# Weight chunks at two alignments, an unscaled first norm and a re-ordered front in a two-block transformer kernel

## The chip, the cores and the metric

One core of one Trainium2 chip. The metric is the device time in microseconds of one execution. Before: 1409.45 us, the median of 3 runs (1404.42 to 1409.93).

## What is computed

Two transformer blocks over 256 tokens of 1024 features, all in float32. Cut to what matters:

```python
def first_block(x, ...):
    h = rms_norm(x, attn_norm)
    mq, mk, mv, dq, dk, dv = split(h @ w_in)             # six parts of 512 columns
    mq, mk, dq, dk = (apply_rope(rms_norm(p, gain), cos, sin) for p in ...)   # norms over heads of 64
    a_out = rms_norm(moba_attention(mq, mk, mv))         # 8 heads
    b_out = rms_norm(diff_attention(dq, dk, dv, lam))    # 4 heads, A1 - lam * A2
    x = x + concat(a_out, b_out) @ w_out
    return x + peer_ffn(rms_norm(x, ffn_norm), ...)      # 16 of 16384 experts for each of 8 heads

def second_block(x, mem, ...):
    h = rmsnorm(x, norm_mix_g)                           # conv, stick-breaking and retention branches,
    x = x + sum(gates * branches) @ w_o                  # from h @ w_in_2
    x = x + memory_attention(rmsnorm(x), rmsnorm(mem, norm_mem_g), w_q, w_kv, w_out)
    x = x + squared_relu_mlp(rmsnorm(x), w_up, w_down)
    return rmsnorm(x, final_g)
```

## The kernel before

Tokens lie on the 128 partitions in two tiles (`TT`). All dense weights come as one stream of 228 chunks of 128 x 1024 float32 (512 KB), in the order of the table `STREAM`. A chunk is loaded by the SP queue into one of `RING` = 4 slots. ACT then writes its rounded high part, `w_hi`, in fp32r (L1009), and POOL the rest, `w_lo = ring - w_hi` (L1360). For six chunks of w_in (3, 5, 9, 13, 17, 21, the list `DVE_CHUNKS`) DVE does the subtraction (L1494), and POOL only sets a mark with a memset (L1376), so that the semaphore `lo_made` counts in order. The activations are split in the same way into `hT_hi` and `hT_lo`. Each product is three fp32r matmuls (`product`, L579 to L581): hi·hi, hi·lo, lo·hi.

There are two kinds of chunk. In a *natural* chunk (w_in 24, w_out 8, xv 8, in_nat 20, w_o 8, xo 8, mlp_down 32) the transposed activations are the stationary operand, which is loaded, and 512 weight columns are moved: 12 matmuls of 512 columns. In a *transposed* chunk (the other 120) the weights are loaded, and 256 columns of `hT` are moved: 24 matmuls of 256. A slot is free for the next `w_hi` when PE has done its chunk (`chunk_done`), and for the next load when its low part is made. In the tensors before, the four slots of `w_hi` and of `w_lo` all start 64 bytes from a multiple of 128; hT and the arena start at a multiple of 128.

Each engine runs its own list, written out in one order, with semaphores between them. PE's results go to 8 PSUM banks, which `plan()` hands out in turn; `open_bank` waits until the last user has emptied a bank. The front of the program, which the change touches, is this:

1. `norm("attn")`: ACT sums the squares of x (L1040), POOL raises the mean to -1/2 (L1344), DVE scales x into `xn` (L1456), PE turns it (L657), ACT and DVE write hT_hi (L1031) and hT_lo (L1450).
2. w_in in six groups of four chunks. For groups 0 to 3 (queries and keys) ACT squares the two results (L1081), DVE sums them over heads of 64 (L1527), POOL raises to -1/2 (L1332, L1334: 128 x 16), and DVE does RoPE: products out of PSUM into `t1` and `t2` (L1540 to L1543), their sum `qn` (L1549), a low part, and the product with the head's factor into `proj1` (L1552, semaphore `roped`). Groups 4 and 5 are values, copied by ACT.
3. `norm("mem")` in the same way for the memory rows; then PE turns the heads into eight `qkT` halves and ACT copies them.
4. Twelve steps of attention (score, maxes, exps, turned probabilities, values), with four chunks of the memory keys (xk) between them, and `keep_busy` matmuls that PE does while it waits.
5. POOL's two powers for the norms of the attention's output (`att_sums`), with low parts around them; then w_out.

From there to the end the change touches only where `w_hi` and `w_lo` lie and how POOL's list is written: in long stretches POOL's low parts run in a `Fori` loop, four to a turn, with the wait in a register.

```python
if made[0] % RING == 0 and loops > 1 and made[0] > max(DVE_CHUNKS):
    with pool.Fori(made[0] // RING, made[0] // RING + loops) as it:
        for s in range(RING):
            lo_part(s, it * RING + s)
```

## Time and profile before

| | us |
|---|---|
| median of 3 runs | 1409.45 |
| lowest, highest | 1404.42, 1409.93 |
| the profiled execution | 1408.7 |
| its span | 1406.9 |
| mean granted TensorE clock | 0.975 |
| PE busy | 1249.2 (89%) |
| POOL busy | 922.4 (66%) |
| DVE busy | 831.0 (59%) |
| ACT busy | 609.8 (43%) |

The span is the profiled stretch, from the first to the last instruction; the time is the whole execution's. PE is TensorE's matmul side and PEld its weight loads, which run beside matmuls. A matmul's duration in the rows holds its pipeline, so neighbours overlap; the distance of two starts tells the pace. `bank` is PSUM, `stat` small per-row numbers, `arena` the big shared SBUF tensor, `c` the constants.

### The profile page before, as it was taken

The numbers are of one execution on the slowest core, as the hardware profiler recorded it, in microseconds if no ns is written. First come the engines' busy times: TensorE is split into PE (matmuls) and PEld (weight loads), VectorE is DVE, ScalarE is ACT, GpSimd is POOL, SyncE is SP. The second block draws the span as 40 slices with busy tenths as digits, with TensorE's granted clock in tenths as the row PEclk, the third lists the DMA queues.
The fourth block names the chain that finished last, engine by engine and source line by source line (L and its number), as shares of the span: only waits on it lengthen the run. The fifth ranks groups of instructions, "written<-read, shape, count | busy, mean of one in ns | idle before, by whom it ended". The sixth has DMA issues, their size and how long they took to land.

```text
span 1406.9 us, 17638 instructions
## 1 busy us (share of the span) xinstructions
PE 1249.2 (89%) x5982; PEld 883.1 (63%) x5982; DVE 831.0 (59%) x1535; ACT 609.8 (43%) x1291; POOL 922.4 (66%) x541
## 2 busy tenths in 40 slices
PE   6999989888888886777878888999999999999997
PEld 5768785443444542233333344789999988899886
DVE  6777478677777767876767654703652632277301
ACT  5456443443534443223233322547455345555432
POOL 5971875555766655644444452896968864799985
PEclk9999999999999999899989999999999999999999
DMA  6540579999999999999999996464536643465662
GB/s 251 162 135 31 186 276 385 426 420 425 427 425 426 425 425 427 427 426 427 428 426 425 413 427 290 141 209 131 186 121 202 210 126 120 135 188 187 203 197 93
DMA packets 72943, 400.69 MB, mean 285 GB/s; under 512 B 8096, under 2 KB 8352, under 8 KB 39712
## 3 DMA queue, kind: packets, MB, share of 16 engines
q0 software_dynamic: 36864, 268.45, 45.5%
q1 hardware_dynamic: 33696, 123.35, 26.6%
q10 hardware_dynamic: 2304, 7.85, 1.5%
q8 instruction: 47, 0.77, 0.2%
q14 instruction: 32, 0.26, 0.0%
HBM read 396.48 MB, written 3.15 MB: 284 GB/s over the span
## 4 chain that ended last, share of the span: by engine, by line
PE 32%; DMA 21%; POOL 18%; issue 16%; DVE 8%; ACT 4%; POOLq 0%; ACTq 0%; SPq 0%; DVEq 0%
DMA arena<-in_experts,arena 21%; POOL w_lo L1360 14%; PE bank L855 11%; PE bank L579 6%; PE bank L581 6%; PE bank L580 6%; DVE arena L1721 3%; POOL arena L1415 2%; POOL stat L1334 1%; PE bank L632 1%; ACT arena L1171 1%; ACT diag L1177 1%; DVE arena L1668 1%; DVE arena L1456 0%; ACT w_hi L1009 0%
## 5 line engine op out<-in xcount | busy, mean ns | idle before, releaser
L1360 POOL TENSOR_TENSOR w_lo<-ring,w_hi 128x1024 fp32r<-128x1024 f32 x222 | 570.6, 2594 | 140.4 <-ACT w_hi L1009 139.4
L855 PE MATMUL bank<-arena,diag 128*128 128x512 f32 x968 | 455.4, 621 | 92.7 <-ACT diag L1177 92.7
L1415 POOL DMA_INDIRECT arena<-in_experts,arena x242 | 294.0, 1215 | 237.9 <-PE bank L855 168.9
L1721 DVE CUSTOM_DVE_ANT_0 arena<-arena 128x1024 f32<-128x1024 f32 x242 | 326.8, 1362 | 165.4 <-DMA arena<-in_experts,arena 165.1
L855 PEld LDWEIGHTS bank<-arena,diag 128*128 128x128 f32 x968 | 184.9, 197 | 342.9 <-issue 203.0
L1009 ACT ACTIVATE w_hi<-ring 128x1024 fp32r<-128x1024 f32 x228 | 240.7, 1059 | 193.2 <-PE bank L581 130.6
L579 PE MATMUL bank<-hT_hi,w_hi 128*128 128x256 f32 x736 | 208.4, 283 | 5.5 <-DVE hT_lo L1450 2.7
L581 PE MATMUL bank<-hT_hi,w_lo 128*128 128x256 f32 x736 | 205.3, 279 | 0.0
L580 PE MATMUL bank<-hT_lo,w_hi 128*128 128x256 f32 x736 | 205.3, 279 | 0.0
L1168 ACT ACTIVATE arena<-arena 128x2 f32<-128x2 f32 (+2 forms) x99 | 20.2, 204 | 410.5 <-DVE arena L1721 410.4
L579 PEld LDWEIGHTS bank<-hT_hi,w_hi 128*128 128x128 f32 x736 | 138.0, 187 | 8.2 <-issue 6.9
L580 PEld LDWEIGHTS bank<-hT_lo,w_hi 128*128 128x128 f32 x736 | 138.3, 188 | 1.0 <-issue 1.0
L581 PEld LDWEIGHTS bank<-hT_hi,w_lo 128*128 128x128 f32 x736 | 138.0, 187 | 0.0
L579 PE MATMUL bank<-w_hi,hT_hi 128*128 128x512 f32 x272 | 115.6, 425 | 9.1 <-POOL stat L1376 3.5
L581 PE MATMUL bank<-w_hi,hT_lo 128*128 128x512 f32 x272 | 108.9, 400 | 0.0
L580 PE MATMUL bank<-w_lo,hT_hi 128*128 128x512 f32 x272 | 108.7, 400 | 0.0
L1177 ACT ACTIVATE diag<-c,arena 128x128 f32<-128x128 f32 x256 | 85.6, 392 | 3.2
L579 PEld LDWEIGHTS bank<-w_hi,hT_hi 128*128 128x128 f32 x272 | 51.9, 191 | 29.4 <-issue 6.9
L1022 ACT ACTIVATE arena<-bank 128x512 f32<-128x512 f32 (+2 forms) x78 | 42.3, 578 | 60.4 <-PE bank L581 38.4
L580 PEld LDWEIGHTS bank<-w_lo,hT_hi 128*128 128x128 f32 x272 | 52.1, 192 | 14.1 <-issue 2.9
L1171 ACT ACTIVATE arena<-arena 128x1 f32<-128x1 f32 x256 | 58.3, 285 | 5.3 <-DVE arena L1715 2.1
L581 PEld LDWEIGHTS bank<-w_hi,hT_lo 128*128 128x128 f32 x272 | 51.8, 190 | 12.8
(243 smaller groups left out, 1694.7 us busy)
## 6 DMA issues: line engine op xcount, KB each, us to landing
ring<-in_stream SPq DMA_DIRECT2D x228, 512.0 KB
arena<-in_experts,arena POOLq DMA_INDIRECT x242
kv_park<-arena ACTq DMA_DIRECT2D x8, 256.0 KB
arena<-kv_park ACTq DMA_DIRECT2D x1, 2048.0 KB, 7.9
x_res<-in_x SPq DMA_DIRECT2D x2, 512.0 KB, 5.2
arena<-in_mem SPq DMA_DIRECT2D x1, 1024.0 KB, 11.3
arena<-in_sub_keys ACTq DMA_DIRECT2D x1, 1024.0 KB, 5.8
out<-arena SPq DMA_DIRECT2D x2, 512.0 KB, 2.6
```

The costliest lines, as they stand in the source:

```text
L579: pe.matmul(out_, stationary[0], moving[0], start=start, stop=False)
L580: pe.matmul(out_, stationary[0], moving[1], start=False, stop=False)
L581: return pe.matmul(out_, stationary[1], moving[0], start=False, stop=stop)
L855: mm = pe.matmul(y_banks[half][:, :], diag[:, slot % DIAGS, :], rows_buf[BUFFER[slot]][:, D + 512 * half:D + 512 * half + 512], start=(i = ...
L1009: nc.scalar.activation(w_hi[:, c % RING, :], ring[:, c % RING, :], ACT.Copy)\
L1022: ins = nc.scalar.activation(dst, bank[:, 0:n] if src is None else src(bank), ACT.Copy, scale=scale)
L1168: own.link(nc.scalar.activation(g, dots[:, slot:slot + count], ACT.Gelu))
L1171: own.mark(nc.scalar.activation(w_slot[:, i % 16:i % 16 + 1], gelus[:, i % 16:i % 16 + 1], ACT.Copy, scale=gates[:, i:i + 1]))
L1177: nc.scalar.activation(diag[:, i % DIAGS, :], ident, ACT.Copy, scale=w_slot[:, i % 16:i % 16 + 1]).then_inc(S("diag_made"), 1)
L1360: nc.gpsimd.tensor_tensor(w_lo[:, slot, :], ring[:, slot, :], w_hi[:, slot, :].bitcast(F32), ALU.subtract).then_inc(S("lo_made"), 1)
L1415: nc.gpsimd.indirect_dma_start(out=rows_buf[b], out_offset=None, in_=experts, in_offset=bass.IndirectOffsetOnAxis(ap=expert_u[:, slot:slot ...
L1721: v.tensor_tensor_reduce(out=rows_buf[b][:, 0:D], in0=xn[:, slot // (PEER_H * PEER_K), :], in1=rows_buf[b][:, 0:D], scale=1.0, scalar=0.0, ...
```

## The change

**Addresses.** `w_hi` and `w_lo` get slots of 1040 words, and `shifted(c)` places chunk c: a natural chunk (`NATURAL`) starts at a multiple of 128 bytes, a transposed one 64 bytes from one, as before. The arena moves below x_res and the constants; the diag tiles start 64 bytes from a multiple of 128 where it was 32.

**First norm.** "attn" joins `UNSCALED`: PE turns x itself. The factor of the rows is left out of queries and keys, where the norm over heads takes it away but for the epsilon (`head_eps`), and is put on the values by ACT's copy.

**Head norms.** POOL's powers go. DVE makes the mean, ACT its square root, and DVE one refining step and a reciprocal. RoPE's first product and the sum stay in PSUM banks 5 and 6, the step in bank 7; w_in takes banks 0 to 4.

**Order.** The turned heads come in `TURN_ORDER`, four halves before the first scores and four after them; the memory norm moves into attention step 0, and ACT scales the memory rows. POOL makes low parts up to `w_out` + 2 before the first attention power, and one more before the second.

**Low parts.** POOL's loop is written out, one instruction to a chunk.

```diff
+HOME = 1040
+NATURAL = ("w_in", "w_out", "xv0", "xv1", "in_nat", "w_o", "xo", "mlp_down")
-UNSCALED = ("ffn", "xa", "mlp")
+UNSCALED = ("attn", "ffn", "xa", "mlp")
+ROPE_BANK, POWER_BANK = 5, 7
...
+            first = key[0] == "w_in" or key[:2] == ("attn", "hT")
+            bank = turn % (4 if among else ROPE_BANK if first else 8)
...
+TURN_ORDER = [(2, 0), (3, 0), (2, 1), (3, 1), (0, 0), (1, 0), (0, 1), (1, 1)]
...
-        line(16)
-        w_hi = tensor("w_hi", [RING, CHUNK], F32R)
-        w_lo = tensor("w_lo", [RING, CHUNK], F32R)
+        line(0)
+        w_hi_mem = tensor("w_hi", [RING * HOME], F32R)
+        w_lo_mem = tensor("w_lo", [RING * HOME], F32R)
...
+            wide = any(FIRST[name] <= c <= LAST[name] for name in NATURAL)
+            return HOME * (c % RING) + (16 if wide == bool(c % 2) else 0)
...
@@ PE
-            norm("attn", xn)
+            norm("attn", xs)
...
+            pe.wait_ge(S("roped"), 4)
+            turn_heads(TURN_ORDER[:4])
...
+                if step == 0:
+                    norm("mem", memn)
+                    turn_heads(TURN_ORDER[4:])
@@ ACT
+                if n < 4:
+                    hi_parts(FIRST["w_in"] + 4 * n + 3 + RING)
+                    act.wait_ge(S("head_means"), n + 1)
+                    nc.scalar.activation(head_root[n], head_mean[n], ACT.Sqrt, scale=0.25).then_inc(S("head_roots"), 1)
...
+            heads_out(TURN_ORDER[:4])
             norm_out("mem", con("g_mem"))
+            heads_out(TURN_ORDER[4:])
@@ POOL
-            for g in range(4):
-                lo_parts(FIRST["w_in"] + 4 * (g + 1) - 1 + RING + 1)
-                pool.wait_ge(S("head_sums"), g + 1)
-                rsqrt(hd_rs[g], hd_ss[g], 1.0 / 64, S("head_rstd"))
-            lo_parts(LAST["w_in"])
+            lo_parts(FIRST["w_in"] + 15)
             norm("mem")
-            lo_parts(LAST["xk"])
+            lo_parts(FIRST["w_out"] + 2)
             pool.wait_ge(S("att_sums"), 1)
             rsqrt(o_rs[:, 16:24], o_ss[:, 16:24], 1.0 / 128, S("att_rstd"))
-            lo_parts(FIRST["w_out"] + 2)
+            lo_parts(FIRST["w_out"] + 3)
@@ DVE
+                low_part(DVE_CHUNKS[2 + g])
...
+                for t in range(TT):
+                    turned = banks[ROPE_BANK + t][:, :]
+                    own.mark(v.tensor_tensor(turned, turned, t2[:, t * 512:(t + 1) * 512], ALU.add))
+                dve.wait_ge(S("head_roots"), g + 1)
+                own.link(v.reciprocal(head_step[g], head_root[g]))
+                own.link(v.scalar_tensor_tensor(head_step[g], head_step[g], 0.25, head_mean[g], ALU.mult, ALU.mult))
+                own.link(v.tensor_tensor(head_step[g], head_step[g], head_root[g], ALU.add))
+                own.link(v.reciprocal(head_power[g], head_step[g]))
```

How the lists move, at three places. First POOL in w_in, groups 1 and 2. Before (L1360 is a low part, L1376 the mark of one by DVE, L1332 and L1334 the power):

```order
L1376 MEMSET stat 128x1 [waits lo_by_dve]
L1360 TENSOR_TENSOR w_lo<-ring,w_hi 128x1024 [waits hi_made] x3
L1332 TENSOR_SCALAR stat<-stat 128x16 [waits head_sums]
L1334 TENSOR_TENSOR stat<-stat 128x16 [waits pool_own]
L1376 MEMSET stat 128x1 [waits lo_by_dve]
L1360 TENSOR_TENSOR w_lo<-ring,w_hi 128x1024 [waits hi_made] x3
L1332 TENSOR_SCALAR stat<-stat 128x16 [waits head_sums]
L1334 TENSOR_TENSOR stat<-stat 128x16 [waits pool_own]
```

and of the change (L1399 a low part, L1409 the mark):

```order
L1409 MEMSET stat 128x1 [waits lo_by_dve]
L1399 TENSOR_TENSOR w_lo<-ring,w_hi 128x1024 [waits hi_made] x3
L1409 MEMSET stat 128x1 [waits lo_by_dve]
L1399 TENSOR_TENSOR w_lo<-ring,w_hi 128x1024 [waits hi_made] x3
L1409 MEMSET stat 128x1 [waits lo_by_dve]
L1399 TENSOR_TENSOR w_lo<-ring,w_hi 128x1024 [waits hi_made] x2
```

The scalings and powers between the low parts are gone; the low parts keep their order.

Second, ACT from the end of w_in to the first exp of the attention. Before (L1031 is the memory norm's hT_hi, L1022 a copy of turned heads, L1098 the exp):

```order
L1031 ACTIVATE hT_hi<-bank,c_55 128x256 [waits result_done]
L1031 ACTIVATE hT_hi<-bank,c_55 128x256
L1031 ACTIVATE hT_hi<-bank,c_55 128x256 [waits result_done]
L1031 ACTIVATE hT_hi<-bank,c_55 128x256
L1031 ACTIVATE hT_hi<-bank,c_55 128x256 [waits result_done]
L1031 ACTIVATE hT_hi<-bank,c_55 128x256
L1031 ACTIVATE hT_hi<-bank,c_55 128x256 [waits result_done]
L1031 ACTIVATE hT_hi<-bank,c_55 128x256
L1022 ACTIVATE arena<-bank 128x512 [waits result_done] x8
L1098 ACTIVATE arena,stat<-arena,stat 128x128 [waits maxes,roped]
```

and of the change (L1048 copies, L1125 the exp of lambda, L1057 the memory norm's hT_hi):

```order
L1125 ACT_TABLE_LOAD
L1125 ACTIVATE stat<-stat 128x2 [waits lam_sums]
L1048 ACTIVATE arena<-bank 128x512 [waits result_done] x4
L1057 ACTIVATE hT_hi<-bank,c_56 128x256 [waits result_done]
L1057 ACTIVATE hT_hi<-bank,c_56 128x256
L1057 ACTIVATE hT_hi<-bank,c_56 128x256 [waits result_done]
L1057 ACTIVATE hT_hi<-bank,c_56 128x256
L1057 ACTIVATE hT_hi<-bank,c_56 128x256 [waits result_done]
L1057 ACTIVATE hT_hi<-bank,c_56 128x256
L1057 ACTIVATE hT_hi<-bank,c_56 128x256 [waits result_done]
L1057 ACTIVATE hT_hi<-bank,c_56 128x256
L1048 ACTIVATE arena<-bank 128x512 [waits result_done] x4
```

A table load and the exp of lambda have come in, and four of the eight copies stand ahead of the memory norm.

Third, POOL between attention and w_out. Before (L1332 and L1334 are the powers of the attention's norms):

```order
L1360 TENSOR_TENSOR w_lo<-ring,w_hi 128x1024 [waits hi_made] x4
L1332 TENSOR_SCALAR stat<-stat 128x8 [waits att_sums]
L1334 TENSOR_TENSOR stat<-stat 128x8 [waits pool_own]
L1360 TENSOR_TENSOR w_lo<-ring,w_hi 128x1024 [waits hi_made] x3
L1332 TENSOR_SCALAR stat<-stat 128x16 [waits att_sums]
L1334 TENSOR_TENSOR stat<-stat 128x16 [waits pool_own]
L1360 TENSOR_TENSOR w_lo<-ring,w_hi 128x1024 [waits hi_made] x6
```

and of the change (L1371 and L1373 the powers):

```order
L1399 TENSOR_TENSOR w_lo<-ring,w_hi 128x1024 [waits hi_made] x9
L1371 TENSOR_SCALAR stat<-stat 128x8 [waits att_sums]
L1373 TENSOR_TENSOR stat<-stat 128x8 [waits pool_own]
L1399 TENSOR_TENSOR w_lo<-ring,w_hi 128x1024 [waits hi_made]
L1371 TENSOR_SCALAR stat<-stat 128x16 [waits att_sums]
L1373 TENSOR_TENSOR stat<-stat 128x16 [waits pool_own]
L1399 TENSOR_TENSOR w_lo<-ring,w_hi 128x1024 [waits hi_made] x5
```

The three low parts that stood between the two powers (chunks 28 to 30) are now ahead of the first, and chunk 31's, which came behind the second, stands between them.

## Rows read from the trace of the kernel before

**Rows 1.** The page, part 1: busy time, share and instructions by engine
```profile
PE 1249.2 (89%) x5982; PEld 883.1 (63%) x5982; DVE 831.0 (59%) x1535; ACT 609.8 (43%) x1291; POOL 922.4 (66%) x541
```

**Rows 2.** Windows of natural-chunk stages: window, length, busy (xcount) by engine, clock, DMA
```profile
14.90:89.10 74.20, 70.59 (x290) 55.38 (x291) 57.96 (x69) 34.50 (x44) 64.71 (x35) 1.00 0.53 171
...
881.40:933.40 52.00, 51.38 (x216) 40.24 (x217) 23.59 (x12) 23.74 (x27) 49.11 (x19) 1.00 0.53 172
1121.50:1146.40 24.90, 22.20 (x88) 17.07 (x87) 10.76 (x13) 8.76 (x11) 14.86 (x7) 0.93 0.40 126
1191.70:1215.30 23.60, 22.87 (x98) 18.02 (x98) 2.96 (x6) 10.37 (x14) 14.68 (x7) 1.00 0.44 134
1309.20:1399.00 89.80, 89.80 (x386) 72.05 (x385) 10.27 (x8) 33.87 (x37) 75.96 (x34) 1.00 0.52 166
```

**Rows 3.** Timeline of PE in mlp_down: start, duration (us), line; thirteen matmuls
```profile
1345.65 0.39 PE L579 MATMUL bank<-w_hi,hidden_hl 128*128 128x512 f32 x1
...
1348.45 0.39 PE L579 MATMUL bank<-w_hi,hidden_hl 128*128 128x512 f32 x1
```

**Rows 4.** Timeline of PE in mlp_up, same columns; thirteen matmuls
```profile
1250.20 0.28 PE L579 MATMUL bank<-hT_hi,w_hi 128*128 128x256 f32 x1
...
1251.61 0.28 PE L579 MATMUL bank<-hT_hi,w_hi 128*128 128x256 f32 x1
```

**Rows 5.** Chain of waits in the gather: start, us, what
```profile
222.69 6.87 PE bank L855 x16
```

**Rows 6.** Timeline of all engines in the first 20 us, same columns
```profile
1.19 1.28 ACT L1040 ACT_TABLE_LOAD   x1 [1.19 <-PEq L2047]
...
5.55 1.06 ACT L1040 ACTIVATE arena<-x_res 128x1024 f32<-128x1024 f32 x1 [3.08 <-DMA x_res<-in_x]
...
8.20 2.25 ACT L1009 ACTIVATE w_hi<-ring 128x1024 fp32r<-128x1024 f32 x2 [0.22 <-DMA ring<-in_stream]
...
9.33 5.11 POOL L1360 TENSOR_TENSOR w_lo<-ring,w_hi 128x1024 fp32r<-128x1024 f32 x2
...
13.02 3.03 ACT L1031 ACTIVATE hT_hi<-bank,c 128x256 fp32r<-128x256 f32 x8 [2.57 <-PE bank L657]
...
14.99 0.76 PE L579 MATMUL bank<-w_hi,hT_hi 128*128 128x512 f32 x1 [0.73 <-DVE hT_lo L1450]
...
16.41 0.63 PE L579 MATMUL bank<-w_hi,hT_hi 128*128 128x512 f32 x1
...
16.83 0.63 PE L580 MATMUL bank<-w_lo,hT_hi 128*128 128x512 f32 x1
```

**Rows 7.** Timeline of POOL in w_in
```profile
53.84 8.10 POOL L1360 TENSOR_TENSOR w_lo<-ring,w_hi 128x1024 fp32r<-128x1024 f32 x3
...
63.17 3.87 POOL L1334 TENSOR_TENSOR stat<-stat 128x16 f32<-128x16 f32 x1
```

**Rows 8.** Timeline of DVE in w_in: the RoPE sum of group 0
```profile
33.47 3.10 DVE L1549 TENSOR_TENSOR arena<-arena 128x1024 f32<-128x1024 f32 x1
```

**Rows 9.** Waits of PE, 15 to 90 us: total, times, longest
```profile
PE bank L579 <- POOL stat L1376: 3.5, 3, 1.6
```

**Rows 10.** Timeline of ACT from w_in to the attention
```profile
94.51 4.06 ACT L1022 ACTIVATE arena<-bank 128x512 f32<-128x512 f32 x8
100.45 0.40 ACT L1098 ACTIVATE arena<-arena,stat 128x128 f32<-128x128 f32 x1 [1.88 <-DVE stat L1581]
```

**Rows 11.** Chain of waits between attention and w_out
```profile
138.00 7.97 POOL w_lo L1360 x3
...
146.34 2.92 POOL stat L1334
...
149.28 3.39 DVE arena L1628
```

**Rows 12.** Timeline of DVE between attention and w_out: the second att_sums
```profile
143.01 1.22 DVE L1622 TENSOR_REDUCE stat<-arena 128x16 f32<-128x1024 f32 x1 [1.21 <-ACT arena L1122]
```

**Rows 13.** Timeline of POOL in in_nat
```profile
884.29 45.87 POOL L1360 TENSOR_TENSOR w_lo<-ring,w_hi 128x1024 fp32r<-128x1024 f32 x17 [7.02 <-ACT w_hi L1009]
```

More of the change, by code:

```diff
@@ L148, in plan @@
     natural("w_in", 6, 4, FIRST["w_in"])
-    norm("mem")
-    for g in range(4):
-        for half in range(2):
-            add(("qkT", g, half))
+    for g, half in TURN_ORDER[:4]:
+        add(("qkT", g, half))
     for step in range(12 + 4):
@@ L161, in plan @@
                 add(("score", m))
+        if step == 0:
+            norm("mem")
+            for g, half in TURN_ORDER[4:]:
+                add(("qkT", g, half))
         if 3 <= step < 15:
@@ L384, in build, with shifted, w_part @@
         lo_mark = stats(6)
+        def shifted(c):
+            wide = any(FIRST[name] <= c <= LAST[name] for name in NATURAL)
+            return HOME * (c % RING) + (16 if wide == bool(c % 2) else 0)
+        def w_part(mem, c, cols=slice(0, CHUNK)):
+            return mem[:, shifted(c) + cols.start:shifted(c) + cols.stop]
         hT = [(hT_hi[:, k, :], hT_lo[:, k, :]) for k in range(KT)]
@@ L405, in build @@
         hd_ss = [stats(16) for _ in range(4)]
-        hd_rs = [stats(16) for _ in range(4)]
         nmax, psums, prec = stats(32), stats(32), stats(32)
@@ L410, in build @@
         ghead = stats(8)
+        head_eps = stats(TT)
+        head_mean, head_root, head_power = ([A(9216 + 64 * i + 16 * g, 16) for g in range(4)] for i in range(3))
+        head_step = [banks[POWER_BANK][:, 16 * g:16 * g + 16] for g in range(4)]
         gain_rows = A(7168, 1024)
@@ L673, in _, with turn_heads @@
             pe.wait_ge(S("c1_loaded"), 16)
-            norm("attn", xn)
+            norm("attn", xs)
             for n in range(6):
                 natural("w_in", 4, n, h_, FIRST["w_in"], normed("attn") if n == 0 else None)
-            norm("mem", memn)
-            for g in range(4):
-                pe.wait_ge(S("roped"), g + 1)
-                for half in range(2):
+            def turn_heads(order):
+                for g, half in order:
                     turn(("qkT", g, half), [proj1[g][:, t, p * P:(p + 1) * P]
                                             for p in (2 * half, 2 * half + 1) for t in range(TT)])
+            pe.wait_ge(S("roped"), 4)
+            turn_heads(TURN_ORDER[:4])
             def score(m, busy=0):
@@ L715, in memory @@
                 transposed_into(xk_bank[:, i % 2 * T:(i % 2 + 1) * T], FIRST["xk"] + i, None, h_)
-            for g in range(4):
-                normed("mem")(g)
             for step in range(16):
                 if step in KEY_STEPS:
+                    if step == KEY_STEPS[0]:
+                        for g in range(4):
+                            normed("mem")(g)
                     if KEY_STEPS.index(step) % 2 == 0:
@@ L1008, in hi_parts @@
                         act.wait_ge(chunk_done, c - RING + 1)
[L1009 removed]
+                    nc.scalar.activation(w_part(w_hi_mem, c), ring[:, c % RING, :], ACT.Copy)\
                       .then_inc(S("hi_made"), 1)
@@ L1462, in norm_low @@
                     split_lo((name, "hT", g), [hT_of[name][k] for k in ks], [gcol[:, k:k + 1] for k in ks])
-            def norm(name, src, dst, gcol):
-                for t in range(TT):
-                    scaled(name, t, src, dst)
-                norm_low(name, gcol)
             def add(key, t, cols):
@@ L1557, in _ @@
             own.link(v.tensor_scalar(lam[:, 5:6], lam[:, 4:5], -LAMBDA_INIT, None, ALU.add))
-            dve.wait_ge(S("mem_loaded"), 16)
-            norm("mem", mem, memn, con("g_mem"))
             mask = o_c2["mask"]
@@ L1582, in _ @@
                          .then_inc(S("maxes"), 1)
+                if step == 0:
+                    norm_low("mem", con("g_mem"))
                 if 1 <= step < 13:
```

99 lines of the change are left out of this document (51 added, 48 removed).

## The prediction

> **What bounds the kernel now.** I read the busy shares first: PE is busy for 89% of the span, POOL for 66%, no engine all the time [rows 1]. So the stages were read one by one in the windows. The middle of the run (about 200 to 870 us) is the expert gather; its DMA is full, and the change does not touch its data. The other stages are a stream of 228 weight chunks, in two kinds. In a *natural* chunk the weights are the moved operand (12 matmuls of 512 columns, 108 chunks), in a *transposed* one they are loaded (24 matmuls of 256 columns, 120 chunks). In the windows of the natural chunks PE is busy for nearly the whole stretch, also where POOL is not: in mlp_down 89.8 of 89.8 us, against 76.0 for POOL [rows 2]. There the spacing of matmuls is the time.
>
> That spacing: twelve natural matmuls start within 2.80 us, 0.2333 us each [rows 3]. At the clock level of 2.4 GHz 512 columns are 0.2133 us, so 0.020 us of each is something else. Twelve transposed matmuls take 1.41 us, 0.1175 each, where 256 columns are 0.1067 [rows 4]. The gather's fp32 matmuls, 512 columns out of addresses that are multiples of 128 bytes, take 6.87 us for sixteen, 0.4294 each, which is two times 0.2147 [rows 5]. At the 1.2 GHz level, in the first microseconds, natural matmuls are 0.42 to 0.43 apart, which is the bare 512 columns [rows 6]. So the extra 9% shows only where fp32r weights are moved at the full clock, from an address 64 bytes off.
>
> **The change part by part.** The sum is made against the profiled execution, 1408.7 us (span 1406.9 and 1.8 around it); the median of the runs shown is 1409.45, 0.75 more.
>
> *1. Start.* Now the squares (5.55), POOL's power, the scaling and two rounds of transposes come before the first matmul at 14.99 [rows 6]. Unscaled, PE turns tile 0 from 5.6 and tile 1 behind it; sixteen transposes are done by about 9. ACT is then the next late one: its first two chunks end at 8.20 + 2.25 = 10.45, and hT_hi follows, eight in 3.03 us, so the first pair at 11.2 and DVE's first low pair (0.9 behind) at 12.1. POOL's second low part ends at 9.33 + 4.7, and the first at 11.7. PE starts at 12.1: **−2.9 us**. Bounds: −1 (POOL's or the ring's order costs more) and −5 (the clock level also rises earlier, since PE turns tiles sooner).
>
> *2. w_in, POOL's powers.* POOL does three low parts in 8.10 us and then a power of 128x16 in 3.87 and its scaling (1.06), 13.1 us for four chunks, where PE needs 4 × 2.80 = 11.2 [rows 7]. PE's waits on this are 3.5 us, three times [rows 9]. The change gives the four powers to ACT (a square root of 16 elements) and DVE (four operations of 16 elements), so POOL has 8.1 us of work in 11.2: **−3.5 us**, bounds 0 and −4. What this puts on DVE: the sum of 1024 was 3.10 us while it read two SBUF operands beside POOL [rows 8] and is now two additions in PSUM of about 0.65, and the product likewise, so DVE's group stays near 10 us, just under PE's pace. Its low part of chunk 4g+9 is needed by PE some 4 us after it is made; that is the cover, and when it is gone PE waits (a rival below). ACT now waits for DVE's means before its next weight part; that part waits for PE for 2.8 us anyway.
>
> ACT also gets two table loads, since Sqrt and Exp alternate: the row of a load is 1.28 us [rows 6]. The first lies beside PE's work. The second stands on the path behind w_in and is in step 3. The Trainium skill (ScalarE: Activation LUTs, Table sets) speaks against this part: it asks to batch by set, since exp and then sqrt are two loads, some 2.66 us each with a drain. By the page step 3 would lose 1.4 us more. The trace has 1.28, and no drain can be told from its rows.
>
> *3. From w_in to attention.* Now the memory norm stands ahead of the heads: first exp at 100.45, 11.7 us behind the last w_in matmul at 88.7 [rows 2, 10]. After: two value copies (1.1), table load and exp (1.5), four copies at 0.51 (row: eight in 4.06), then PE's scores and sixteen transposes of mem, ACT's eight hT_hi (3.03) and four more copies, and then the first exp, at +11 to +12.5. PE however is ahead in the order: its scores and transposes of step 0 are done by +9.7, where all of them end at about +13 now, and it has less to wait for. The two nearly cancel: **−0.5 us**, bounds −2 and +2.6.
>
> *4. w_out.* POOL makes three w_out low parts (7.97) between the two powers, and the second power, the wait of DVE's scaling, starts only at 146.34 [rows 11]. After, these three are made in POOL's idle time before the first power and one, chunk 31's, of 2.4 us stands between; it can be done when DVE's second sums are, at 143.01 + 1.22 [rows 12]. **−2.0 us**, bounds 0 and −2.5.
>
> *5. Moved weights at a multiple of 128 bytes.* No row has an fp32r matmul of 512 columns moved from there. Bounds: 0.2147, the pace of one pass in rows 5, as the best, and 0.2533, the excess of 0.020 once more, as the worst, if the loaded hT at a multiple of 128 and the moved weights then meet in the memory. I take 0.2147: it is the nearest row with 512 columns moved from such an address. That is 12 × 0.0186 = 0.223 us a chunk: w_in 24 chunks −5.4; w_out 6 (two lie under a wait) −1.3; in_nat −3.0, as POOL's 17 low parts take 45.87 us from 884.29 on [rows 13], 2.70 each, so the last in_nat one ends at 927.5 and PE cannot end before 930.4 (now 933.4); w_o 7 −1.6; xo 8 −1.8; mlp_down 32 −7.1. Eight chunks of xv in the gather: 0, the gather's DMA covers them. **−20.1 us**. In mlp_down a chunk would take 2.58 and POOL's low part is 2.40 where DVE is quiet, so POOL is next, close behind.
>
> The Trainium skill (TensorE: Matmul & The Clock Gate, Back-to-back issue gap) gives N/2.4 + 2.5 ns, 0.2158 us for 512 columns, and knows no address. By the page the term would be 18.9 and not 20.1. Rows 3 disagree with it by 0.0175.
>
> *6. Loop written out, and the rest.* POOL's registers and branches go; low parts follow each other as closely without the loop (8.10 for three) as in it (45.87 for 17, beside DVE) [rows 7, 13]. 0. The diag tile starts 64 and not 32 bytes off; the gather waits for DMA, not for its weight load. 0.
>
> Sum: −2.9 − 3.5 − 0.5 − 2.0 − 20.1 = −29.0, so 1408.7 − 29.0 = 1379.7, and as a median 1380 us.
>
> **The rivals.**
>
> *A, the forecast*: 1380, with its own range 1371 to 1390, the low end by a start of −5, an attention of −2 and some better pace, the high one if half of step 5 comes.
>
> *B, the address does nothing for the moved operand.* For it: the transposed matmuls move hT from a multiple of 128 and yet are 10% over their columns [rows 4], so the excess may belong to fp32r at the full clock. Against: there the load of 128 columns takes as long as the matmul and can be the cause; in natural chunks it has twice the room, and the excess is there all the same. Then 1408.7 − 8.9 = 1400, with 1395 to 1405.
>
> *C, slower.* Loaded and moved operand both at a multiple of 128 collide. Now they are always 64 bytes apart, in both kinds, and this may be what keeps the excess at 9%. At 0.2533 each of some 95 chunks on the path costs 0.24 more, 22.8 us: 1408.7 − 8.9 + 22.8 = 1423. It decides from 0.2333 + 8.9/1140 = 0.241 us a matmul on; below that the front's gain pays for it. For it speaks only that the spacing is so regular; against it, that nothing in rows 5 suffers, though diag is loaded meanwhile.
>
> *D, DVE becomes the bound of w_in.* It keeps 10 to 12 us a group (RoPE through PSUM, four dependent small operations, a low part, the sum, the product) against PE's 10.3. If it needs 12.5, the low parts 17 and 21 come late and PE waits about 5 us: 1385, inside the range of A.
>
> *E, the front gives nothing* (the start bound by the ring's DMA, the root's wait holding ACT's weight parts): 1389 with step 5, 1409 without it.
>
> **How the numbers follow.** A with D 0.52, B 0.33, C 0.10, E without step 5 0.05. The measurement can tell about 0.5%, 7 us, from no change. Faster than 1402.4: A, most of B (0.30) and a slice of C and E (0.02): 0.84. Within 0.5%: the rest of B and E, 0.07. Slower: C, 0.09. The range takes A and most of B, **1371 to 1403**.
>
> **What would show it.** Spacing of twelve natural matmuls in mlp_down: 2.58 (A), 2.80 (B), over 2.9 (C). First w_in matmul near 12.1; no wait of PE on POOL's memset in w_in, whose last matmul is at about 76 (A) or 81 (B); spacing of transposed matmuls still 0.1175. First exp 11 to 12.5 behind w_in. Second att power near 144.3 less the front's gain. mlp_down from first to last 82 us and not 89. The forecast is wrong if the natural spacing stays, or if PE waits for low parts by DVE in w_in.

## The result and the profile after

The changed kernel takes 1417.7 us (median of 7 runs, 1414.91 to 1420.44) against 1409.45 (7 runs, 1404.42 to 1413.33): ratio 1.0052, 95% interval 1.0035 to 1.0069. It is half a per cent slower, where 1380 us (1371 to 1403) were forecast. Its profiled execution took 1417.7 us with a span of 1415.9; before, the span was 1406.9, so there are 9.0 us to find.

The page of the changed kernel, part 1, answers to [rows 1]:

```profile
PE 1256.9 (89%) x5982; PEld 890.4 (63%) x5982; DVE 829.5 (59%) x1564; ACT 614.1 (43%) x1299; POOL 892.0 (63%) x533
```

The shares say nothing: POOL is 30 us less busy, and the kernel is slower all the same. The windows by stage do tell. (in_gate is here the first 12 of its 24 chunks, up to a pause of 9.9 us that all the kernels have.) Columns as in [rows 2]; of the changed kernel w_in, in_nat, in_gate, w_o, xo, mlp_down, and last the gather from the first dot to the last:

```profile
12.30:80.50 68.20, 68.06 (x290) 55.39 (x291) 54.85 (x97) 37.74 (x50) 46.36 (x29) 0.98 0.63 203
881.40:933.40 52.00, 51.14 (x218) 40.17 (x219) 23.89 (x12) 23.81 (x27) 49.05 (x19) 1.00 0.55 171
998.10:1041.00 42.90, 35.87 (x293) 35.68 (x292) 30.87 (x21) 16.60 (x22) 28.75 (x12) 0.88 0.44 143
1124.80:1155.90 31.10, 25.66 (x100) 20.09 (x99) 14.24 (x15) 9.79 (x12) 17.03 (x8) 0.89 0.39 119
1202.00:1225.50 23.50, 22.72 (x100) 18.15 (x99) 3.01 (x6) 10.35 (x14) 14.75 (x7) 1.00 0.44 135
1319.20:1408.00 88.80, 88.80 (x387) 72.08 (x385) 10.63 (x8) 33.84 (x37) 76.27 (x34) 1.00 0.54 168
...
199.50:869.80 670.30, 561.70 (x1501) 270.90 (x1501) 475.73 (x1059) 240.34 (x721) 362.19 (x275) 0.93 1.00 416
```

The same two stretches of the kernel before that were not among its rows, in_gate and the gather:

```profile
999.20:1034.60 35.40, 34.62 (x293) 34.42 (x292) 25.86 (x21) 16.62 (x23) 31.12 (x12) 1.00 0.51 168
...
206.40:869.80 663.40, 551.95 (x1501) 265.55 (x1501) 478.25 (x1060) 240.45 (x721) 365.31 (x275) 0.95 1.00 420
```

Read one below the other: w_in is 6 us shorter than in [rows 2]. The gather begins 6.9 us sooner (199.5 against 206.4) and is 6.9 us longer, so its last dot starts at 869.8 in both kernels: the front's whole gain is gone there, at a full DMA that moves 416 GB/s instead of 420. in_gate is 7.5 us longer at a granted clock of 0.88, and w_o, from first to last matmul, 30.7 us against 26.9 (the window of [rows 2] begins inside the stage). From first to last matmul xo is 0.2 shorter and mlp_down 1.1. Stage by stage the books close: before in_gate −1.1, in_gate +7.6, up to w_o −0.8, w_o +3.8, up to mlp_down +0.7, mlp_down −1.1, together +9.1 of the 9.0.

Inside in_gate one wait does it, shown by the waits of all engines from 1015 to 1030 us (waiting engine and line, what it waited for, total, times, longest), and the chain there (start, us, what):

```profile
PE bank L596 <- DVE arena L1880: 7.0, 1, 7.0
```

```profile
996.59 4.96 DVE arena L1859
1001.57 3.48 DVE arena L1862 x4
1005.07 6.01 DVE arena L1866 x4
1011.11 8.27 DVE arena L1870 x4
1019.41 3.32 DVE arena L1873
1022.75 2.72 DVE conv_hl L1874
...
1026.64 0.56 DVE arena L1880
1027.24 0.58 PE bank L596
1027.82 0.21 PE bank L597
1028.03 0.21 PE bank L598
```

PE waits for a bank that holds the retention scores (L1880). DVE empties it only after its whole convolution, because that is the order of its program. The convolution's operations of 254 columns take 0.48 us alone and 2.6 when they meet a POOL low part: L1870 is four of them in 8.27 us. After the gap the matmuls are 0.21 us apart and not 0.113: the 1.2 GHz level. In w_o it is the same pair of engines, on DVE's timeline (start, us, what):

```profile
1118.93 2.52 DVE L1934 CAST hT_hi<-arena 128x512 fp32r<-128x512 f32 x1
1121.49 2.78 DVE L1935 TENSOR_TENSOR hT_lo<-arena,hT_hi 128x512 fp32r<-128x512 f32 x1
...
1124.90 2.19 DVE L1931 TENSOR_TENSOR arena<-arena 128x512 f32<-128x512 f32 x1
1127.13 2.47 DVE L1934 CAST hT_hi<-arena 128x512 fp32r<-128x512 f32 x1
1129.64 2.71 DVE L1935 TENSOR_TENSOR hT_lo<-arena,hT_hi 128x512 fp32r<-128x512 f32 x1
```

and on PE's, where the last three rows are 0.43 apart (the 1.2 GHz level again, as in [rows 6]):

```profile
1132.50 0.77 PE L596 MATMUL bank<-w_hi,hT_hi 128*128 128x512 f32 x1 [4.66 <-DVE hT_lo L1935]
1133.06 0.63 PE L597 MATMUL bank<-w_lo,hT_hi 128*128 128x512 f32 x1
1133.49 0.63 PE L598 MATMUL bank<-w_hi,hT_lo 128*128 128x512 f32 x1
```

Last, the spacing of mlp_down, answering to [rows 3], one matmul in three:

```profile
1351.27 0.39 PE L596 MATMUL bank<-w_hi,hidden_hl 128*128 128x512 f32 x1
...
1353.98 0.39 PE L596 MATMUL bank<-w_hi,hidden_hl 128*128 128x512 f32 x1
...
1356.74 0.40 PE L596 MATMUL bank<-w_hi,hidden_hl 128*128 128x512 f32 x1
...
1359.54 0.40 PE L596 MATMUL bank<-w_hi,hidden_hl 128*128 128x512 f32 x1
```

Twelve matmuls take 2.71 us in one place and 2.80 in another. Averaged by chunk, the whole stage repeats with a period of four chunks: 226.7, 232.7, 233.3, 227.9 ns. (The first matmul or two of a chunk still have the spacing of the chunk before, hence 227.9 and 232.7.) Four is the number of ring slots, so the spacing belongs to the slot, two quick and two slow.

### The profile page after: what moved, and what is told of

It is laid out like the page before. It is cut to its first block, busy times and chain, and to the rows that moved or that the text cites. A ratio compares the mean times of both kernels' runs of the same rounds, so it can differ in the third digit from the quotient of the medians.

```text
span 1415.9 us, 17416 instructions
## 1 busy us (share of the span) xinstructions
PE 1256.9 (89%) x5982; PEld 890.4 (63%) x5982; DVE 829.5 (59%) x1564; ACT 614.1 (43%) x1299; POOL 892.0 (63%) x533
## 4 chain that ended last, share of the span: by engine, by line
PE 51%; DMA 20%; DVE 12%; POOL 8%; ACT 5%; issue 4%; ACTq 0%; SPq 0%; POOLq 0%; DVEq 0%
DMA arena<-in_experts,arena 20%; PE bank L881 11%; PE bank L596 11%; PE bank L598 11%; PE bank L597 11%; POOL w_lo L1399 5%; DVE arena L1761 4%; POOL arena L1443 2%; PE bank L649 1%; PE bank L658 1%; ACT w_hi L1035 1%; ACT arena L1210 1%; ACT diag L1216 1%; PE bank L1006 1%; DVE arena L1870 1%
## 5 line engine op out<-in xcount | busy, mean ns | idle before, releaser
L1399 POOL TENSOR_TENSOR w_lo<-ring,w_hi 128x1024 fp32r<-128x1024 f32 x222 | 564.7, 2568 | 190.5 <-ACT w_hi L1035 189.8
L881 PE MATMUL bank<-arena,diag 128*128 128x512 f32 x968 | 466.7, 635 | 91.1 <-ACT diag L1216 91.0
L1443 POOL DMA_INDIRECT arena<-in_experts,arena x242 | 288.5, 1192 | 247.2 <-PE bank L881 171.2
L1761 DVE CUSTOM_DVE_ANT_0 arena<-arena 128x1024 f32<-128x1024 f32 x242 | 322.1, 1343 | 174.5 <-DMA arena<-in_experts,arena 174.3
L881 PEld LDWEIGHTS bank<-arena,diag 128*128 128x128 f32 x968 | 190.3, 202 | 347.5 <-issue 213.0
L1048 ACT ACTIVATE arena<-bank 128x512 f32<-128x512 f32 (+2 forms) x74 | 40.2, 570 | 59.1 <-PE bank L598 39.9
L598 PEld LDWEIGHTS bank<-w_hi,hT_lo 128*128 128x128 f32 x272 | 52.0, 191 | 12.1
```

What stands on the lines that cost most here:

```text
L598: return pe.matmul(out_, stationary[1], moving[0], start=False, stop=stop)
L881: mm = pe.matmul(y_banks[half][:, :], diag[:, slot % DIAGS, :], rows_buf[BUFFER[slot]][:, D + 512 * half:D + 512 * half + 512], start=(i = ...
L1048: ins = nc.scalar.activation(dst, bank[:, 0:n] if src is None else src(bank), ACT.Copy, scale=scale)
L1399: nc.gpsimd.tensor_tensor(w_part(w_lo_mem, c), ring[:, c % RING, :], w_part(w_hi_mem, c).bitcast(F32), ALU.subtract).then_inc(S("lo_made"), 1)
L1443: nc.gpsimd.indirect_dma_start(out=rows_buf[b], out_offset=None, in_=experts, in_offset=bass.IndirectOffsetOnAxis(ap=expert_u[:, slot:slot ...
L1761: v.tensor_tensor_reduce(out=rows_buf[b][:, 0:D], in0=xn[:, slot // (PEER_H * PEER_K), :], in1=rows_buf[b][:, 0:D], scale=1.0, scalar=0.0, ...
```

## The experiments

Twelve kernels in three groups, each measured beside the kernel before on the same chip. A reader of the texts on record needs one convention: addresses "modulo 256 bytes" are counted there from the kernel's first array. In the built program that array lies at 16512, itself 128 bytes past a multiple of 256, so "128 modulo 256" there is a true multiple of 256, and "a multiple of 256" there is 128 bytes off. Differences between two addresses are not touched by this.

| kernel | edit | this, us | before, us | ratio, interval |
|---|---|---|---|---|
| e1_all64 | changed, all chunks at 64 | 1418.74 | 1411.01 | 1.0056, 1.0043 to 1.0069 |
| e2_all128 | changed, all chunks at 0 | 1412.94 | 1411.01 | 1.0010, 1.0001 to 1.0019 |
| e4_all64_loop | e1 with POOL's loop | 1416.25 | 1411.01 | 1.0047, 1.0028 to 1.0065 |
| e5_arena | changed, arena 128 bytes on | 1405.59 | 1411.01 | 0.9956, 0.9941 to 0.9970 |
| b1_before_arena | before, arena 128 bytes on | 1419.24 | 1409.83 | 1.0069, 1.0046 to 1.0091 |
| e3_before_written | before, loop written out | 1411.36 | 1409.83 | 1.0008, 0.9996 to 1.0019 |
| e6_same256 | e5, moved chunks at the residue of hT | 1400.94 | 1409.83 | 0.9949, 0.9929 to 0.9969 |
| e7_pause | e5, one pause of POOL | 1403.10 | 1409.83 | 0.9957, 0.9941 to 0.9972 |
| e8_pause3 | e6, three pauses of POOL | 1397.74 | 1411.11 | 0.9909, 0.9889 to 0.9929 |
| e9_rs_first | e6, DVE's order in in_gate | 1397.55 | 1411.11 | 0.9914, 0.9901 to 0.9926 |
| e10_both | e8 and e9 | 1391.01 | 1411.11 | 0.9872, 0.9855 to 0.9889 |
| e11_front_alone | front only, layout of before | 1404.23 | 1411.11 | 0.9960, 0.9947 to 0.9973 |

### The place of the arena

The change moves the 128 KB arena ahead of x_res, and with it the buffers that the gathered rows land in. The edit of **e5_arena**:

```diff
+        place[0] += 32
         arena_at = place[0]
         arena = tensor("arena", [32768])
```

> The changed kernel with the arena, into which the gathered rows land, moved by 128 bytes in SBUF, to the same residue (128 modulo 256 bytes) as before the change. Arena theory: an 8192-byte packet of the gather goes back from 314 to 310 ns and the last dot from 869.8 to about 863 us, so the total to about 1410. Run-to-run theory (the transfers' rate belongs to the run or the chip): packets stay where those of the other kernels of this call are, total within 2 us of 1417.7.

The last dot is at 862.1 us, where 863 was expected, 7.7 sooner than in the changed kernel. The ratio falls by more, from 1.0052 to 0.9956: in_gate took 39.0 us in this profile and 42.5 in that one, which belongs to the stalls below. Beside it **b1_before_arena**, the same step in the other direction in the kernel before:

```diff
-        line(0)
+        line(32)
         arena_at = place[0]
```

> The kernel before with only its arena moved on by 128 bytes, from 128 modulo 256 bytes to a multiple of 256. Arena theory: the gather's 8192-byte packets go from 310 to 314 ns, the last dot from 869.8 to 877 to 879 us, the total to about 1416 to 1418 (in mlp_down the spacing may fall, next sentence). Residue theory of the spacing (a moved chunk is quick when its address modulo 256 bytes less that of the loaded operand is 0 or 64, slow at 128 or 192): mlp_down, whose hidden rows lie in the arena, goes from .2333 to .2290, -1.6 us; in_nat, whose operand is not in the arena, stays .2333. If the front was what slowed the gather: 1409 to 1411.

It came as the arena theory had it: 1419.24 us, last dot at 880.5. (It also starts the gather 2.2 us late, at 208.6.) The stretch from the first dot to the last, over all profiled runs:

| arena | kernels | first to last dot, us |
|---|---|---|
| at a true multiple of 256 bytes | before, e3, e5 to e11 | 661.7 to 663.4 |
| 128 bytes off | changed, b1, e1, e2, e4 | 670.4 to 672.9 |

Fourteen traces, no overlap, about 9 us apart. Windows of b1 and of e5 over the gather (columns as above):

```profile
208.50:881.80 673.30, 555.03 (x1504) 267.25 (x1504) 481.59 (x1061) 241.35 (x724) 365.92 (x275) 0.94 1.00 414
```

```profile
199.20:863.40 664.20, 555.11 (x1505) 267.96 (x1504) 481.64 (x1061) 241.30 (x723) 360.22 (x275) 0.94 1.00 420
```

The busy times of PE, DVE and ACT are the same to 0.1 us (POOL's, which also issues the gather, differs by 5.7); the length and the GB/s differ. The packets of 8192 bytes, 33,061 to 33,064 in each trace, take on average over the run 0.3156 us in the changed kernel and in b1, 0.3121 before, 0.3117 in e5 and 0.3114 in e11. The Trainium skill (DMA: Bandwidth & Descriptors, How a descriptor splits into AXI transactions) says, in words about reads, that a descriptor is cut at multiples of 256 bytes and that one which starts off such a multiple fetches from the multiple below it. If a landing address counts in the same way, an 8192-byte row takes 33 transactions and not 32, an estimate of up to 3%. The traces agree in direction, with 1.1% a packet; where in the transfer it is lost, no run here shows.

### The addresses of moved and loaded operands

**e1_all64** and **e2_all128** put all chunks at one offset:

```diff
-            return HOME * (c % RING) + (16 if wide == bool(c % 2) else 0)
+            return HOME * (c % RING) + (0 if c % 2 else 16)
```

and for e2 the last line reads

```diff
+            return HOME * (c % RING) + (16 if c % 2 else 0)
```

> The changed kernel with every split chunk 64 bytes from a multiple of 128, as before the change; all else as changed. Loop theory (POOL's written-out low parts shift its phase against DVE and hold the convolution and the w_o stage): nothing comes back by this, 1417 to 1420, mean matmul spacing of mlp_down .2333. Address theory (the mixed addresses themselves upset the stages): 1405 to 1410, with the 7.2 us gap before in_gate's end (1019.9 us) gone. My term 5 as measured in the changed kernel's trace (.2300 against .2333 where operands move) says 2 to 3 us slower than the changed kernel: 1420.

> The changed kernel with every split chunk at a multiple of 128. If the address acts only on chunks that are moved, the natural stages keep .2300 and the transposed ones (chunk loaded) keep .1133 to .1178: time within 2 us of 1417.7. If an address at the multiple hurts the loaded chunk, mlp_up's mean spacing grows over .1178 and the time by 1 us per 1.1 per cent of its 90 us.

e1: 1418.74, so nothing comes back, and the address theory of the stage losses falls. But mlp_down repeats 229.2, 228.9, 232.4, 233.3 ns over its four chunks, which .2333 everywhere (my expectation) is not. e2: natural chunks as in the changed kernel, but transposed ones went to 118.5 to 120.0 ns on average, and mlp_up to 91.8 us from 90.3: a *loaded* chunk at a multiple of 128 bytes is slower by 1.7%. By slots it is about 118.5 in 1 and 2, which lie 128 bytes from the moved hT modulo 256, and about 119.9 in 0 and 3, which lie at distance 0. hT itself is at a multiple of 128 in every kernel, so no run parts the chunk's own address from its distance to hT. (e2's median is nevertheless lower than e1's. Its profiled run has no stall in in_gate, and the runs of e1 scatter by 10 us; see below.)

The quick slots are known by one number: the address of the moved chunk less that of the loaded operand, modulo 256 bytes.

| difference | seen in | ns a matmul |
|---|---|---|
| 0 | changed, slots 0 and 3; e5, slots 1 and 2; e6, all | 226.7 |
| 64 | e1, slots 0 and 1; b1's mlp_down, all | 228.9 |
| 128 | changed, slots 1 and 2; e5, slots 0 and 3 | 233.3 |
| 192 | before, all; e1, slots 2 and 3 | 233.3 |

The slots are 4160 bytes apart in the changed kernel, 64 more than a multiple of 256, so offsets that are all multiples of 128 are still two residues modulo 256. In e5 the hidden rows moved by 128 bytes and quick and slow slots changed places. b1 had been foretold: its hidden rows moved from difference 192 to 64, .2290 expected, .2289 measured. The last step was **e6_same256**, with every natural chunk at difference 0:

```diff
-HOME = 1040
+HOME = 1024
...
-        line(0)
-        w_hi_mem = tensor("w_hi", [RING * HOME], F32R)
-        w_lo_mem = tensor("w_lo", [RING * HOME], F32R)
-        line(0)
+        place[0] += 32
+        w_hi_mem = tensor("w_hi", [RING * HOME + 16], F32R)
+        place[0] += 48
+        w_lo_mem = tensor("w_lo", [RING * HOME + 16], F32R)
+        place[0] += 48
...
-            return HOME * (c % RING) + (16 if wide == bool(c % 2) else 0)
+            return HOME * (c % RING) + (0 if wide else 16)
...
-                        act.wait_ge(chunk_done, c - RING + 1)
+                        act.wait_ge(chunk_done, c - RING + 1 + int(c % RING < 3 and shifted(c) > shifted(c - RING)))
```

The added words put w_hi, w_lo, hT and the arena all at one residue. A transposed chunk reaches 64 bytes into the next slot, so ACT waits for one chunk more where such a chunk follows a natural one.

> The changed kernel with the arena at 128 modulo 256 bytes, and every moved chunk, in all four slots, at the same residue modulo 256 as the operand loaded beside it (loaded chunks 64 bytes further; the slots no longer spread by 64 bytes). Residue theory: spacing .2267 in all slots of mlp_down (after: .2267 in two slots of four, .2333 in the two others), mlp_down 87.1 to 87.3 us against 88.3, all natural stages together -3 us: about 1402. If the alternation over the slots has another cause (the 4160-byte stride, the bank): still .2300 on average, 1405 to 1406.

All slots of mlp_down stand at .2267 from the fifth chunk on. Two rows of its timeline, twelve matmuls apart:

```profile
1345.34 0.39 PE L598 MATMUL bank<-w_hi,hidden_hl 128*128 128x512 f32 x1
...
1348.06 0.39 PE L598 MATMUL bank<-w_hi,hidden_hl 128*128 128x512 f32 x1
```

mlp_down is 87.1 us from first to last matmul (changed 88.3, before 89.4), and the median 1400.94. The ratios of e6 and e5, 0.9949 and 0.9956, are not told apart; what shows the rule is the spacing and the length of the stage.

### The written-out loop and the front, each alone

**e4_all64_loop** is e1 with the removed Fori loop back; **e3_before_written** is the kernel before without it:

```diff
-                    loops = (last + 1 - made[0]) // RING
-                    if made[0] % RING == 0 and loops > 1 and made[0] > max(DVE_CHUNKS):
-                        with pool.Fori(made[0] // RING, made[0] // RING + loops) as it:
...
-                        made[0] += RING * loops
-                    elif made[0] in DVE_CHUNKS:
+                    if made[0] in DVE_CHUNKS:
```

> The changed kernel with every chunk at 64 bytes and with POOL's loop for the low parts back: what is left of the change is the unscaled front and the place of the arena. Loop theory: the gap before in_gate's end goes from 7.2 to about 1 us and the w_o stage's losses (3.8 us) go, leaving only the slower gather against the front's gain: 1406 to 1410. If the loop is innocent (phase by the front): like e1, 1417 to 1420.

> The kernel before with POOL's low parts written out and nothing else. My term 6: 0, so 1409 to 1412 beside a before of 1411. Rival (the written-out row is quicker to start and so holds DVE's convolution longer): in_gate's gap grows from 0.9 to 4 to 7 us, 1415 to 1418.

e4 is 1416.25 (e1: 1418.74) and e3 has 1.0008, with 1 in its interval; e3's gap in in_gate (the longest distance of two matmuls less the usual one) is 0.93 us, before 0.94. The loop is innocent, and my first theory of the stage losses falls with it. e4's seven runs go from 1408.6 to 1421.0, e1's from 1410.2 to 1420.2, far more scatter than the 5.7 us over 18 runs of the kernel before on the same chip. The profiled runs of both were the fastest, and their in_gate had a gap of 0 (e4) and 1.4 us (e1), not 7.

**e11_front_alone** keeps all that the change does to the front; chunks, strides and loop are those of before, and so is the residue of every array modulo 256 bytes but that of the diag tiles (192 for 160). The arena stays ahead of x_res, at a true multiple of 256.

> The unscaled front alone: chunks, low-part loop and the residues of every array modulo 256 bytes as in the kernel before. My terms 1 to 4 give -8.9; the changed kernel's trace has the gather begin 6.9 us sooner, so 1403 beside a before of 1410, last dot at 863. If the front itself costs something later (another phase of POOL against DVE), the gain at the gather is there and part of it is lost behind 930 us: 1405 to 1410.

1404.23 against 1411.11, −6.9 us: most of what the front gives at the gather is kept to the end. In the profiled executions it is −7.3 at the first dot (199.1), −9.0 at the last (860.8) and −5.5 at the end of the span; w_o is 1.4 us longer, as it is in e3. The gap in in_gate is 0.92 us, as before. So the front alone does not bring the two long stalls; the rest of the change took its gain.

### DVE against POOL's low parts

**e7_pause** takes e5 and makes POOL wait once:

```diff
                 pool.wait_ge(S("hi_made"), c + 1)
+                if c == FIRST["w_o"] + 2:
+                    pool.wait_ge(S("merged"), 4)
```

> The kernel e5_arena with one wait more: POOL makes the low part of w_o's third chunk only when DVE has made all four pairs of merged rows. Port theory (a DVE operation of 0.43 to 0.69 us that meets a POOL low part takes 2.5 to 2.8 us, and this alone makes the gap of 4.7 us in w_o and the half clock behind it): DVE's operations there take 0.43 to 0.69 us, the gap goes, 1398 to 1400. If DVE is late there for another reason: gap stays over 4 us, or a wait on low parts takes its place, 1405 or more.

DVE's timeline of e7 in that stage, with POOL silent from 1109.9 to 1118.1:

```profile
1113.55 0.69 DVE L1934 TENSOR_TENSOR arena<-arena 128x512 f32<-128x512 f32 x1
1114.28 0.43 DVE L1937 CAST hT_hi<-arena 128x512 fp32r<-128x512 f32 x1
1114.74 0.69 DVE L1938 TENSOR_TENSOR hT_lo<-arena,hT_hi 128x512 fp32r<-128x512 f32 x1
```

The three took 2.19, 2.47 and 2.71 us in the changed kernel. The port theory of the durations is right, and my price for the fix was wrong: the time is 1403.1 and not 1398 to 1400, and by the ratios (0.9957, e5 0.9956) the pause gained nothing, because a wait on the low part takes the place of the wait on DVE:

```profile
PE bank L597 <- POOL w_lo L1402: 4.4, 2, 3.6
```

PE is through with the second chunk at 1116.5, and POOL may start the third one's low part only at 1117.9. The Trainium skill (SBUF — State Buffer, Who interferes with whom) says that a DVE instruction with two SBUF inputs, or a copy in a fast mode, and a GpSimd instruction that reads SBUF shut each other out for a whole instruction. The rows agree: 0.43 becomes 2.5 us, which is POOL's 2.4, and the evacuation that reads a PSUM bank (0.68) is never stretched. Hence **e8_pause3**, on top of e6, with POOL's pauses only as long as PE can bear:

```diff
+                if 2 <= c - FIRST["w_o"] <= 4:
+                    pool.wait_ge(S("merged"), c - FIRST["w_o"])
```

> The kernel e6_same256 with POOL's low parts of w_o's third, fourth and fifth chunks each waiting for DVE's pair of merged rows of that number less one (2, 3 and 4 pairs made), instead of e7's one wait for all four. Port theory: every DVE operation of a pair is 0.4 to 0.7 us or held once at most, no gap over 1.5 us in w_o, no half clock there, w_o 24 to 25.5 us against 29.8: 5 us off, about 1397. If low parts then come too late (as e7's gap of 3.8 us shows can be), the gap only moves: 1400 to 1402.

w_o is 26.1 us from first to last matmul (e6: 29.8), its longest gap 1.47 and its granted clock 1.00; the median is 1397.74, and by the ratios it is 0.4% under e6. The expected 5 us came as 3.7 in the stage. Its profiled run was one of 1405.93 us and had the other stall: PE waits 7.2 us in in_gate.

**e9_rs_first** goes at that one, by DVE's order alone:

```diff
+            for h in range(4):
+                bank = take(dve, ("rs", h))
+                v.tensor_tensor(sT[:, h, :], bank[:, 0:SC], o_c3["decay"][:, h * SC:(h + 1) * SC], ALU.mult)\
+                 .then_inc(evac_sem(("rs", h)), 1)
             for c in range(6):
                 wait_evacuated(dve, ("in_conv", c))
             u = cv[:, 1]
...
-            for h in range(4):
-                bank = take(dve, ("rs", h))
-                v.tensor_tensor(sT[:, h, :], bank[:, 0:SC], o_c3["decay"][:, h * SC:(h + 1) * SC], ALU.mult)\
-                 .then_inc(evac_sem(("rs", h)), 1)
```

> The kernel e6_same256 with DVE's four evacuations of the retention scores moved ahead of its convolution. Order theory (in_gate's gap of 1 to 7 us, different from run to run, is PE waiting for a bank that DVE frees only behind the convolution, whose operations POOL's low parts hold): no gap in in_gate over 0.3 us, and e6's two groups of times (1398 to 1401, 1406 to 1408) become one: 1397 to 1400. If the gap has another releaser it stays, with both groups.

1397.55, five runs between 1396.81 and 1400.23, where e6 had ten in two groups (six at 1398.1 to 1401.2 and four at 1406.0 to 1407.9). Five runs alone could miss the slower group by luck; the trace is the better witness: no gap is left in in_gate. The convolution is as slow as it was, but nobody waits for it.

> Both edits of e8_pause3 and e9_rs_first together. If they touch different stalls they add up: 1392 to 1395. If the time saved at one comes back as another wait, no better than the better of the two.

**e10_both**, the two edits together: 1391.01, ratio 0.9872. They add up. Windows of in_gate and w_o:

```profile
987.70:1020.70 33.00, 33.00 (x293) 33.00 (x292) 32.69 (x19) 16.64 (x22) 29.36 (x12) 1.00 0.57 185
1105.30:1131.90 26.60, 23.45 (x101) 17.84 (x100) 11.58 (x14) 8.76 (x11) 15.71 (x7) 1.00 0.43 135
```

PE is busy 33.0 of 33.0 us in in_gate (changed: 35.87 of 42.90), and the clock is 1.00 in both stages (changed: 0.88 and 0.89). DVE is busy for 32.69 us in in_gate, more than in the changed kernel (30.87), and it costs nothing. This version beats both kernels: 1.3% under the one before.

## Why the prediction was wrong

The forecast was −29.0 us, the profiled executions differ by +9.0, and 38 us are to be accounted for. About 17 of them are step 5, 11.4 are two stalls that no step had, 6.9 are the gather, and about 3 are the front. Step by step:

- **1, the start** (−2.9): first w_in matmul at 12.44, forecast 12.1, −2.55. Right. The clock's earlier rise, which was in the bounds only, came too: the matmuls 0.427 apart end at 15.5 and not at 19.4, some 0.7 us inside w_in.
- **2, POOL's powers** (−3.5): PE's waits on POOL in w_in [rows 9] are gone, 3.5 us. Right. Rival D, DVE as the bound of w_in, did not come: PE has no gap over 0.6 us between 12.44 and 80.06.
- **3, w_in to attention** (−0.5, bounds −2 and +2.6): wrong in size and sign. The first exp is at 92.90, 12.8 behind the last w_in matmul (forecast 11 to 12.5, before 11.7), and then the clock fell, which I had not in the sum. The window from 92.9 to 105.0 has a granted clock of 0.72, the same stretch before 1.00:

```profile
92.90:105.00 12.10, 12.10 (x59) 9.16 (x58) 6.36 (x19) 5.16 (x20) 2.41 (x1) 0.72 0.15 43
```

```profile
100.45:110.00 9.55, 9.55 (x57) 7.02 (x57) 7.13 (x22) 4.49 (x15) 2.42 (x1) 1.00 0.09 24
```

  0.28 × 12.1 = 3.4 us, and the lead over the kernel before shrinks from 8.7 at the end of w_in to 4.6 at DVE's second att sums (138.37 against 143.01): step 3 is +4, of which 1.1 is the later exp and the rest the clock. The fall does not come in every execution. Of the eleven profiled kernels with the new front, e1, e7 and e10 kept 1.00 from w_in to w_out; the window 80 to 140 us of the changed kernel and of e1:

```profile
80.00:140.00 60.00, 55.60 (x366) 45.98 (x366) 40.35 (x106) 39.04 (x109) 17.33 (x11) 0.94 0.23 71
```

```profile
80.00:140.00 60.00, 55.58 (x380) 46.21 (x379) 41.57 (x109) 39.35 (x110) 20.57 (x11) 1.00 0.25 81
```

  These three start the first dot at 196.9 to 197.8, the other eight at 199.1 to 200.6. Ahead of the exp PE waited 0.52 and 1.35 us in the changed kernel, and just as long in e1 and e7, so those two waits do not decide it. What does was not found.
- **4, w_out** (−2.0): the second power now starts 0.1 us behind the end of its sums (139.68). Before, it stood 1.8 behind them, low parts in between (146.05 in POOL's timeline against 144.23 [rows 12]): −1.7. Right.

  Up to here 8.9 were forecast without the address. At the first dot 6.9 arrive, of which about 1.2 is the address's (w_in and w_out), so the front gave 5.7 in this execution. e11, which has the front alone, is 6.9 us faster at the end.

- **The sentence that failed** stands outside the numbered terms: "its DMA is full, and the change does not touch its data". It moves the arena, and so the start of every gathered row, off a multiple of 256 bytes: +6.9 us here, about 9 between the two groups of traces. I had read that line of the diff as bookkeeping and priced it at nothing without a sentence. e5 and b1 show it in both directions.
- **5, the address** (−20.1): mis-sized by its row and wrong in its rule. I took .2147 from fp32 matmuls [rows 5]; fp32r ones stood at .2267 at best. (The formula that the prediction takes from the Trainium skill, TensorE: Matmul & The Clock Gate, Back-to-back issue gap, is given on that page for an isolated matmul and not for a stream, so it was no ground for this term.) And what counts is not the address of the moved chunk but its distance from the loaded operand's, modulo 256: the changed kernel has the good distance in half its slots only. Measured, the mean spacing of the natural stages fell from 233.3 to between 230.2 and 230.9 ns: −0.9 us for the 288 matmuls of w_in, −0.3 in w_out, −0.2 in each of in_nat (PE's busy time), w_o and xo, −1.1 in mlp_down, about −3 in all. e6 about doubles it. Rival B (nothing, .2333) was nearer. The time lies near rival C's 1423, but by luck: its cause (collision, over .241) did not come for moved chunks; e2 shows something of the kind, in small, for the loaded ones.
- **6, the loop** (0): right, e3.
- **What was in no step**: in_gate +7.6 and w_o +3.8. Both stalls were there before ([rows 2] has w_o at a clock of 0.93, and in_gate had a gap of 0.9 us); they hang on how DVE's short operations and POOL's low parts happen to meet. That DVE's order makes the one and POOL's low parts the other is shown by e9 and e8. Why they grew goes by the pace of the transposed chunks, as far as traces tell: 113.3 ns a matmul for long stretches and not 117.8, so that a chunk takes 2.72 us and leaves 0.3 us beside POOL's 2.4, where it was 2.83 and 0.4. In w_o all eleven traces without a pause of POOL agree: the longest gap is 4.7 to 4.9 us where the chunks ahead of w_o ended at 113.3 (changed, b1, e1, e4, e5, e6, e9), and 2.1 to 2.2 where they ran at 117.8 or slower (before, e2, e3, e11). b1 is the kernel before with its arena moved, so w_o's stall does not need the changed chunks. In in_gate the gap is 0.9 to 1.1 with the first eight chunks at 117.8 (before, b1, e3, e11, e6), 4.1 and 4.4 with four of them at 113.3 (e7, e5) and 7.2 and 7.4 with all eight (changed, e8), but 1.4 and 0 in e1 and e4, which also ran all eight at 113.3; e2, at 118.5 to 120.0, has 0.1. So this link is read from traces, has two exceptions and was not tested by itself, and what picks the pace stays open.

In one line: −6.9 at the first dot, +6.9 in the gather, +11.4 in the two stalls, and −2.3 in all other stages.

## What to carry to other kernels

When an edit reorders a memory layout, list every array whose address moves and who touches it, DMAs first: here one line moved the landing place of 268 MB, and 128 bytes cost 9 us. Where a matmul's pace matters, look at it chunk by chunk; a period equal to the number of buffers points at their addresses, and the average hides it. And before a stage is priced by its steady pace, ask which stall in it depends on the meeting of two engines: put what PE waits for ahead of what nobody waits for in the other engine's order, and let a helper that runs ahead pause while the late one works.

## What was not expected of the hardware

- Matmuls of fp32r with 512 moved columns are 226.7, 228.9, 233.3 and 233.3 ns apart as moved less loaded address is 0, 64, 128 and 192 modulo 256 bytes.
- Those with 256 moved columns have two paces, 113.3 and 117.8 ns, in one and the same kernel with one and the same layout. The kernel before runs the fifth to the eleventh chunk of mlp_up at 113.3 and all from the twelfth on at 117.8, and in in_conv it goes from 113.3 to 117.8 behind the fourth chunk. There each change stands at a break of PE's stream, of 0.03 to 0.55 us; but the changed kernel also goes from 117.8 to 113.3 at the end of the fourth chunk of in_sqk, where no distance is over 0.12 us. With the loaded chunk at a multiple of 128 bytes (e2) both are gone and it is 118.5 to 120.0. What picks one of the two was not found.
- In w_o a longest gap of 2.1 to 2.2 us left the granted clock at 1.00 in e2, e3 and e11, and one of 2.1 was followed by the 1.2 GHz level in the kernel before (0.93 in [rows 2]), so the length of the gap alone doesn't tell. One of 3.8 (e7) and those of 4.7 to 4.9 (changed, b1, e1, e4, e5, e6, e9) were all followed by it (0.88 to 0.94 over the stage).
